# Placing the turned activations of a split-precision transformer kernel at 128-byte starts in SBUF

## The reference

```python
z = jnp.matmul(h, w_in)                                   # 1024 -> 3200, two layers
x = x + rms_norm(jnp.matmul(y, w_out), g_mix_post)        # 1024 -> 1024
gate, up = jnp.split(jnp.matmul(h, w_gate_up), [FFN_HIDDEN], axis=-1)   # 1024 -> 5632
f = jnp.matmul(jax.nn.silu(gate) * up, w_down)            # 2816 -> 1024
# second block, latent tokens and 256 context tokens:
... = h_lat @ w_in ; ... = h_ctx @ w_in                   # 1024 -> 2208, then 2560
```

## Time and profile before

| | us |
|---|---|
| median of 3 runs | 1123.51 (1123.21 to 1123.52) |
| the profiled execution, its own time | 1121.75 |
| span of the profiled execution, first to last instruction | 1119.9 |
| PE busy | 1086.1 (97%) |
| PEld busy (overlaps PE) | 883.6 (79%) |
| DVE busy | 683.9 (61%) |
| ACT busy | 554.7 (50%) |

### The profile page before, as it was taken

One profiled execution on the slowest core, in us unless ns is written; L12 is line 12 of the kernel. 1 busy time (PEld: TensorE's weight loads), 2 busy tenths in 40 slices (PEclk: granted clock), 3 DMA queues, 4 the chain that ended last, 5 costly groups with the idle time before them and its releaser, 6 DMA issues.

```text
span 1119.9 us, 15597 instructions
## 1 busy us (share of the span) xinstructions
PE 1086.1 (97%) x5974; PEld 883.6 (79%) x5974; DVE 683.9 (61%) x1198; ACT 554.7 (50%) x999; POOL 77.2 (7%) x94
## 2 busy tenths in 40 slices
PE   7999999999999999999999999999998999999997
PEld 5889776688886988776688778889796678889785
DVE  5986665566545786575566547523256753876664
ACT  5654364455435554364455445334235642534772
POOL 1000110000002000110000000001000002021040
PEclk9999999999999999999999999999999999999999
DMA  9644576665666744486876485223211012443001
GB/s 300 218 141 151 173 241 192 219 211 186 188 188 203 242 139 152 143 280 211 256 235 183 153 323 153 73 87 107 75 58 57 1 57 57 132 142 122 2 1 38
DMA packets 109716, 170.46 MB, mean 152 GB/s; under 512 B 7229, under 2 KB 70730, under 8 KB 109386
## 3 DMA queue, kind: packets, MB, share of 16 engines
q1 hardware_dynamic: 107668, 161.95, 45.8%
q0 software_dynamic: 1440, 6.10, 1.6%
q10 hardware_dynamic: 534, 1.41, 0.3%
HBM read 168.39 MB, written 1.05 MB: 151 GB/s over the span
## 4 chain that ended last, share of the span: by engine, by line
PE 84%; DVE 8%; ACT 4%; issue 3%; DMA 1%; POOL 0%; SPq 0%; DVEq 0%; POOLq 0%; ACTq 0%
PE PS L477 16%; PE PS L478 15%; PE PS L479 15%; PE PS L2997 4%; PE PS L2998 4%; PE PS L2999 4%; PE PS L977 3%; PE PS L1810 1%; DVE low L450 1%; PE PS L941 1%; PE PS L942 1%; PE PS L943 1%; PE PS L1484 1%; ACT high L440 1%; PE PS L1798 1%
## 5 line engine op out<-in xcount | busy, mean ns | idle before, releaser
L450 DVE TENSOR_TENSOR low<-raw,high 128x1024 fp32r<-128x1024 f32 (+3 forms) x182 | 202.2, 1116 | 190.8 <-ACT high L440 189.9
L477 PE MATMUL PS<-high,hT_high 128*128 128x512 f32 (+2 forms) x796 | 308.0, 387 | 4.3 <-DVE low L450 2.0
L478 PE MATMUL PS<-low,hT_high 128*128 128x512 f32 (+2 forms) x796 | 299.5, 376 | 0.0
L479 PE MATMUL PS<-high,hT_low 128*128 128x512 f32 (+2 forms) x796 | 299.4, 376 | 0.0
L440 ACT ACTIVATE high<-raw 128x1024 fp32r<-128x1024 f32 (+3 forms) x186 | 179.6, 972 | 221.1 <-PE PS L479 123.4
L477 PEld LDWEIGHTS PS<-high,hT_high 128*128 128x128 f32 x796 | 150.6, 189 | 49.5 <-issue 15.0
L453 DVE SCALAR_TENSOR_TENSOR low<-raw,vec_cols,high 128x512 fp32r<-128x512 f32 x176 | 124.2, 747 | 75.3 <-ACT high L443 75.2
L479 PEld LDWEIGHTS PS<-high,hT_low 128*128 128x128 f32 x796 | 150.5, 189 | 24.2
L478 PEld LDWEIGHTS PS<-low,hT_high 128*128 128x128 f32 x796 | 150.8, 189 | 21.7
L443 ACT ACTIVATE high<-raw,vec_cols 128x512 fp32r<-128x512 f32 x176 | 117.1, 714 | 73.9 <-PE PS L479 38.5
L2997 PE MATMUL PS<-high,fT_high 128*128 128x512 f32 x176 | 70.4, 400 | 0.0
(11 more groups left out here) (377 smaller groups left out, 1602.0 us busy)
## 6 DMA issues: line engine op xcount, KB each, us to landing
raw<-w_gate_up SPq DMA_DIRECT2D x176, 256.0 KB
raw<-w_mod SPq DMA_DIRECT2D x48, 512.0 KB
raw<-w_down SPq DMA_DIRECT2D x44, 512.0 KB
raw<-w_in SPq DMA_DIRECT2D x56, 384.0 KB
raw<-o_w_in SPq DMA_DIRECT2D x20, 512.0 KB
raw<-w_out SPq DMA_DIRECT2D x16, 512.0 KB
raw<-e_w_in SPq DMA_DIRECT2D x12, 512.0 KB
raw<-w_in SPq DMA_DIRECT2D x8, 512.0 KB
```

Source lines behind the costliest of these rows:

```text
L450: last = e.tensor_tensor(g.low, g.raw, g.high.bitcast(F32), ALU.subtract)
L477: e.matmul(bank, xh[:, k, tokens], g.high[:, i, :], start=first and i == 0, stop=False)
L478: e.matmul(bank, xh[:, k, tokens], g.low[:, i, :], start=False, stop=False)
L479: done = e.matmul(bank, xl[:, k, tokens], g.high[:, i, :], start=False, stop=last and i == len(g.rows) - 1)
```

## The change

The pair `hT_high`, `hT_low` is declared directly behind the tiles `low`, ahead of `consts`, and `half_power` is declared with 24 columns where it had 16. Nothing else is touched: the same instructions run in the same order on the same engines, on tiles at other places.

```diff
         high = [sb(f"high{i}", [P, SLOT], F32R) for i in range(CUT)]
         low = [sb(f"low{i}", [P, SLOT], F32R) for i in range(CUT)]
+        hT_high = sb("hT_high", [P, DK, SEQ], F32R)
+        hT_low = sb("hT_low", [P, DK, SEQ], F32R)
         consts = sb("consts", [P, a["const_early"].shape[1]])
...
         prob = xn_flat[:, 768:1920].rearrange("p (b s) -> p b s", b=3)
-        hT_high = sb("hT_high", [P, DK, SEQ], F32R)
-        hT_low = sb("hT_low", [P, DK, SEQ], F32R)
...
-        half_power = sb("half_power", [P, 16])
+        half_power = sb("half_power", [P, 24])
```

## The result

| | before | after |
|---|---|---|
| median of 4 executions, us | 1123.36 (1121.22 to 1123.52) | 1111.29 (1109.01 to 1112.21) |
| the profiled execution, us | 1121.75 | 1109.01 |
| its span, us | 1119.9 | 1107.2 |
| PE busy, us | 1086.1 | 1072.4 |

The ratio after to before is 0.9894, with a 95% interval of 0.9874 to 0.9914: the kernel became 1.1% faster, 12 to 13 us. The profiled executions are 1.6 and 2.3 us under the medians of their kernels. The forecast was 1123.0 us, the range 1117.8 to 1127.3, and no rival named this time.

A forecast was written before the change was run, and what follows sets the result against it. TensorE's matmul stream was taken to bound the kernel (PE busy 1086.1 of 1119.9 us). All terms were 0 except cT's 0.5 us: 1121.75 - 0.5 = 1121.25, carried to the median as 1123.0 us; range 1117.8 to 1127.3.

The forecast's parts named there:

- Steps 1 to 4: Instructions, VectorE/ScalarE/DMA work, fp32 transposes, and the load of the stationary operand: each priced at 0.
- Step 2: VectorE, ScalarE, DMA: same operations at other starts; DVE groups L453 and L643 take 747 and 748 ns; price 0.
- Step 4: Stationary operand's load: 188 to 189 ns at any start, hidden under the 233 ns between 512-column starts; price 0.
- Step 5: Distance between split-product matmul starts: cT leaving 96 gains 0.5 us; fT 0; hT from 32 to 0 taken as 0.
- B: Split products: the whole surplus over the columns' time comes from unaligned starts; 58 us gained, 1065 us; chance 0.04.
- what would show it: Signs: unchanged 233.3 to 233.5 and 173.5 ns, cT blocks falling to hT's, loads 188 ns, PE busy within 2 us.
- the hT term of step 5: hT products, 1584 of 512 and 756 of 384 columns, moved from 32 to 0: taken as 0, bounds 4.1 us either way.
- the fT term: fT products of 512 columns, moved from 96 to 0: 0 gained, by the long stretches.
- Rival A: Split products: start at 0 beats 32 as much as 32 beats 96; 5.1 us gained, 1118.4 us; chance 0.26.
- Rival C: hT products in all layer stages: both streams on the same phase collide; 4.1 us slower, 1127.6 us; chance 0.18.
- D: x_now, xn, silu_c stay off 128, so transposes and modulation keep their starts; sum unchanged; chance 0.52 together with the forecast.

## Why the prediction was wrong, point by point

**What bounds the kernel** was right: PE's stream alone set the time, and 13.7 us on PE became 12.7 us of span.

**Steps 1 to 4** (instructions, VectorE and DMA, transposes, the length of the load) were right at 0 for what they name. The 16 transposes from kT (L2190) take 1.75 us with kT at 0, as they did at 96. Step 2 read its row L453 a little wrong, since vec_cols in it begins at 32; with o_gained of L643 moved from 96 to 0 both groups take 748 ns. The load stays at 188 to 189 ns. Step 4's reason, that the load is hidden because it is shorter than the distance, was too simple: loads of the same length go with 226.7 and with 233.3 ns, and a load of 134 ns takes the distance to 230 from either side.

**Step 5 failed**, in three ways. First, it priced the move to 0 by the step between 32 and 96, as if the start of the stationary operand were the quantity. The runs with all at 32 (whole gain) and with the weights at 32 (none) show that the difference to the moving operand is. Seen so, 32 and 96 were two unequal cases, and their small step (1.2 and 2.9 ns) said nothing about the equal one, 5.5 to 7.1 ns away at 512 columns. Second, it took the 256-column products for the nearest rows with the new state. They had the stationary operand at 0 and the moving one at 32, so they were unequal as well. The prediction said under B that no product had both aligned, and under "what would show it" that this was the combination no row had; it should have let the bounds of step 5 go there, since the surplus itself, 20 ns on 2352 matmuls and 13.5 on 840, stood open as 58 us. Third, the long stretches of fT and hT at one and the same 233.3 to 233.5 ns were read as a sign that the start doesn't matter once the stream runs. Both had unequal starts, 224 and 32 bytes apart, and 64 and 96 gave the same 233.3 to 233.8 ns in the runs above; equal starts have another value, 226.7. In terms of the sum, the hT term of step 5 was put at 0 and measured 7.8 us at 512 columns (with the few of `w_out`), and the fT term was put at 0 and measured 3.1.

**Rival A** had the sign and neither mechanism nor size: it expected the 384-column products of hT near 171 ns, and they stayed at 173.6; it gave 5.1 us for 12.7. **Rival B** had the cause (starts) and was too large: 6.6 of the 20 ns at 512 columns went, almost none at 384, and 256 got worse by 2. **Rival C** named the right relation, both streams beginning on the same phase, and the wrong sign: equal phase is the good case, except at 256 columns. **D** was right in that x_now and silu_c change nothing of the sum: their products and transposes took as long as before.

The observations named ahead of time decide it well: cT's blocks at 384 columns fell to hT's 2.08 us as forecast, which was luck, since the reason was the equal starts and at 512 columns they fell by 7.1 ns a matmul and not by 1.2; and PE's busy time moved by 13.7 us where under 2 was expected.

"TensorE: Matmul & The Clock Gate" of the Trainium skill (Step-by-step: what each phase is for) says that loading the next tile's weights doesn't steal SBUF read bandwidth from the running matmul. The runs agree in so far as half a load does not give back half of the surplus. But load and stream are not independent: the place of the loaded operand moves the distance by 6.4 ns in the stretch of fT, and half a load moves it by 3.1 ns one way or 2.4 ns the other. The gap of 216 ns for 512 columns in its section Back-to-back issue gap was not held over a stretch at any start tried; the best was 226.7.

## What to carry to other kernels

Where a kernel is bound by a stream of matmuls, read the distance from start to start in undisturbed stretches, by width, and compare it with the columns at the granted clock: a surplus that is the same for tiles at different places can still come from their places, if all of them differ from the other operand's start. For long runs of fp32r products of 512 columns with a fresh stationary operand each time, place the stationary tiles at the same remainder modulo 256 bytes as the moving ones; a multiple of 128 for one of them is neither needed nor enough. The products of 256 columns lost by it here, so count both kinds first. Before taking a row as the nearest case of a new state, write down all operands of that row and of the new state, not only the one that the change names.

## What the runs showed of the hardware that was not expected

- At 512 columns, 128x128 stationary, fp32r, the distance settles to a value that holds for a whole stretch. With starts equal modulo 256 bytes it is 226.7 ns (226.9 to 227.7 over stretches with their beginnings), with differences of 32, 64, 96 and 224 it is 233.3 to 233.8; 128 gives 232.3, and 16 gives 226.7 or 233.3 from stretch to stretch.
- It takes some matmuls to get there. The timeline of PE in the kernel after, in the first matmuls behind a transpose step of the first feed-forward stage (start, us):

```profile
192.23 0.40 PE L478 MATMUL PS<-low,hT_high 128*128 128x512 f32 x1
...
193.62 0.39 PE L478 MATMUL PS<-low,hT_high 128*128 128x512 f32 x1
...
194.31 0.39 PE L478 MATMUL PS<-low,hT_high 128*128 128x512 f32 x1
...
194.99 0.39 PE L478 MATMUL PS<-low,hT_high 128*128 128x512 f32 x1
```

  the first six distances take 1.39 us (232 ns each), the next three 0.69 (230) and the three after them 0.68 (227). Short stretches between gaps therefore gain less, which is why hT (227.7) gains less than fT (226.9). The scores of the grouped attention (L1927 and L1928: 512 columns, o_q stationary, the keys in cT moving, both behind wsT and so 0 apart) had equal starts already in the kernel before. They stand in rows of at most four between narrower matmuls, and behind the first of a row most are 228 to 240 ns apart in both kernels.
- With equal starts a matmul takes 13.3 to 13.6 ns over its columns at 512, 384 and 256 columns alike. For 256 columns that is more than the 11 ns in the kernel before, where activation and weights were 32 bytes apart. But unequal is not always better there: in the run with the weights at 32, hT 96 bytes from them, the 95 distances from 1011.09 us on take 11.40 us, 120.0 ns each, as with equal starts. The lowest value of all is that of hT 16 bytes off: from 1002.94 us on, 95 distances take 10.79 us, 113.5 ns each, while the next stretch of the same kernel has 118.7. So which placement narrow products want is open.
- With equal starts a smaller stationary operand makes the stream of 512 columns slower (230.0 ns with 64 columns, 231.5 with 32, 226.7 with 128); with unequal starts 64 columns make it faster (230.9 for 233.3). Why load and stream fall into these cycles, and why smaller loads lose the good one, is not settled by these runs.
